# Three seams of a two-block transformer kernel: part-wise waits for weights, products placed inside two mixers, and an end in two token halves

## Time and profile before

| | us |
|---|---|
| median of 3 runs (2592.61 to 2595.39) | 2592.93 |
| the profiled execution | 2590.93 |
| its span, first to last instruction | 2588.8 |
| PE busy | 2524.4 (98%) |
| DVE busy | 1324.3 (51%) |
| ACT busy | 562.1 (22%) |
| POOL busy | 1516.1 (59%) |

### The profile page before, as it was taken

How to read it: one execution, slowest core, us unless ns; L and a number is a source line. 1 busy time by engine, 2 the same in 40 slices (tenths; PEclk the granted TensorE clock), 3 DMA queues, 4 the chain that set the end, 5 groups by cost and what they waited for, 6 DMA issues and landing times.

```text
span 2588.8 us, 31978 instructions
## 1 busy us (share of the span) xinstructions
PE 2524.4 (98%) x11898; PEld 2052.7 (79%) x11898; DVE 1324.3 (51%) x1550; ACT 562.1 (22%) x1022; POOL 1516.1 (59%) x854
## 2 busy tenths in 40 slices
PE   8999999999999999999999999999999978999997
PEld 6888887778888888888887778888887766888886
DVE  5555527656555315555147656555336655655512
ACT  2110014652111001110015552110113554111000
POOL 5666665436666666666665436666664322666664
PEclk9999999999999999999999999999999999999999
DMA  4222221102222222222221112232222110222222
GB/s 154 97 97 97 98 98 66 66 33 98 97 97 97 98 98 84 95 97 97 98 98 66 51 48 98 97 121 97 98 98 114 53 47 33 97 96 93 93 97 76
DMA packets 34915, 228.65 MB, mean 88 GB/s; under 512 B 5392, under 2 KB 6288, under 8 KB 8080
## 3 DMA queue, kind: packets, MB, share of 16 engines
q1 hardware_dynamic: 33392, 225.92, 24.5%
q10 hardware_dynamic: 1440, 1.55, 0.2%
HBM read 225.36 MB, written 2.10 MB: 88 GB/s over the span
## 4 chain that ended last, share of the span: by engine, by line
PE 92%; DVE 4%; ACT 1%; issue 1%; POOL 1%; DMA 0%; SPq 0%; DVEq 0%; POOLq 0%; ACTq 0%
PE bank L571 27%; PE bank L573 27%; PE bank L572 27%; PE bank L700 2%; PE bank L685 1%; PE bank L592 1%; PE bank L669 1%; PE bank L670 1%; POOL wl L542 1%; PE bank L928 1%; PE bank L913 1%; PE bank L586 1%; PE bank L587 1%; DVE ropet L1524 1%; DVE rstd L1425 0%
## 5 line engine op out<-in xcount | busy, mean ns | idle before, releaser
L542 POOL TENSOR_TENSOR wl<-raw,wh 128x1024 fp32r<-128x1024 f32 x412 | 1036.4, 2516 | 34.4
L539 POOL TENSOR_SCALAR wh<-raw 128x1024 fp32r<-128x1024 f32 x412 | 444.4, 1079 | 1012.3 <-PE bank L573 965.4
L571 PE MATMUL bank<-xh,wh 128*128 128x512 f32 x2096 | 818.6, 391 | 0.0
L572 PE MATMUL bank<-xl,wh 128*128 128x512 f32 x2096 | 816.5, 390 | 0.0
L573 PE MATMUL bank<-xh,wl 128*128 128x512 f32 x2096 | 816.3, 389 | 0.0
L573 PEld LDWEIGHTS bank<-xh,wl 128*128 128x128 f32 x2096 | 393.6, 188 | 83.1
L571 PEld LDWEIGHTS bank<-xh,wh 128*128 128x128 f32 x2096 | 393.6, 188 | 80.7
L572 PEld LDWEIGHTS bank<-xl,wh 128*128 128x128 f32 x2096 | 393.7, 188 | 80.6
L571 PE MATMUL bank<-acth,wh 128*128 128x512 f32 x880 | 342.3, 389 | 0.0
L572 PE MATMUL bank<-actl,wh 128*128 128x512 f32 x880 | 342.3, 389 | 0.0
L573 PE MATMUL bank<-acth,wl 128*128 128x512 f32 x880 | 342.3, 389 | 0.0
(11 more groups left out here) (247 smaller groups left out, 2357.4 us busy)
## 6 DMA issues: line engine op xcount, KB each, us to landing
raw<-in_stream SPq DMA_DIRECT2D x206, 1024.0 KB, 4.8
x<-in_x SPq DMA_DIRECT2D x4, 512.0 KB, 7.4
w1k<-in_w1k SPq DMA_DIRECT2D x1, 2048.0 KB, 9.3
out_dram<-x SPq DMA_DIRECT2D x4, 512.0 KB, 2.7
w1v_low<-in_w1v SPq DMA_DIRECT2D x1, 1024.0 KB, 6.9
w1v_high<-in_w1v SPq DMA_DIRECT2D x1, 1024.0 KB, 9.0
...
```

Of the source, the lines that this page charges most:

```text
L539: nc.gpsimd.tensor_scalar(wh[:, h, :, :], src, 1.0, 1.0, ALU.mult, ALU.mult)\
L542: nc.gpsimd.tensor_tensor(wl[:, h, :, :], src, wh[:, h, :, :].bitcast(F32), ALU.subtract).then_inc(split_done, 1)
L571: mm = nc.tensor.matmul(bank, wh[:, slot, k, :], rh, start=start, stop=False)
L572: mm = nc.tensor.matmul(bank, wh[:, slot, k, :], rl, start=False, stop=False)
```

## The change

- `first_units`: PE waits for the high part of unit 1 only, makes six of its high-by-high products, then waits for the low part, makes two low ones, and goes on as before with the rest behind.
- First mixer: at step 1 of the first pair the fill stands before the scores. In the last pair five blocks of the output projection's tile 0 (and a sixth and seventh behind the last transposes) stand between the steps, in the order in which their inputs come; `pooled_map` and what follows it on ACT and DVE move from steps 4 to 8 to steps 1 to 6, through bank 1 alone.
- Second mixer: the units are done at G=44 (`FILL2`: three blocks at 14 steps, and 1, 1, 3, 3 at steps 41 to 44), with the last query unit last. On DVE, `blocks2(0)` stands before the loop and `blocks2(1)` at step 1; `keys2(5)` is cut in two (G=4, 5). The gelu of v goes from G=32 to 30, the transposes to 33 to 36, mean and root from 41/42 to 38, `scale_gated` from DVE at 43 and 45 to ACT at 39, `spatial` from 46 to 49 to 40 to 43, the gelu of u from 50 to 42, `gated` from 52/53 to 45/46, `add_a` from 54/55 to 47/48, `token_sums` from 56 to 49, `norm_rows` from 60 to 52, `normed` from 61/62 to 53/54, `low_mix` from 63 and later to 55/56. The second group's compressed branch goes later: scores from 41/43 to 44/48, minimum 44 to 49, `compressed_normalise` 47 to 51, `compressed_turn` 51 to 54. `queries2(3)` goes from G=38 to 45. At G=56 to 63 stands one block of `out_half(0)` each.
- The end: the last tile's product is made in two halves of 256 tokens in two banks. The squares of the first seven tiles are summed over channels before it is done (`partial_sums`); for each half only column sums of 128x2 go through mean, root and reciprocal, which are spread and transposed to rows. DVE scales six tiles of each half, POOL two (ACT has multiplied their gains in before), and five transfers by SyncE and one by ACT send the halves out.

```diff
-ORDER2 = [12, 13, 14, 8, 15, 16, 17, 9, 4, 5, 6, 10, 7, 0, 11, 1, 2, 3]
+ORDER2 = [12, 13, 14, 8, 15, 16, 17, 9, 4, 5, 6, 10, 7, 0, 1, 2, 3, 11]
...
-FILL2 = tuple(2 + (G in (10, 18, 26, 34, 42, 47)) if G < 49 else 0 for G in range(STEPS2))
+FILL2 = tuple(2 + (G in (9, 12, 15, 18, 21, 24, 27, 29, 31, 33, 35, 37, 39, 40)) if G < 41 else (1, 1, 3, 3)[G - 41]
+              if G < 45 else 0 for G in range(STEPS2))
...
-Q_UNIT = (3, 7, 11, 14)
+Q_UNIT = (3, 7, 11, 17)
 GV_UNIT = (8, 9, 10, 12)
-GU_UNIT = (13, 15, 16, 17)
+GU_UNIT = (13, 14, 15, 16)
...
-          "rows1", "scores0", "scores1", "rows2", "weights0", "blocks0", "blocks1", "gated0", "gated1", "rows3",
-          "gated2", "gated3", "scores2", "scores3", "rows4", "spatial0", "spatial1", "spatial2", "spatial3",
-          "weights1", "rows5", "blocks2", "rows6", "blocks3", "rows7", "sums", "norm_rows"]
+          "rows1", "scores0", "scores1", "rows2", "weights0", "blocks0", "gated0", "gated1", "gated2", "gated3", "rows3",
+          "blocks1", "spatial0", "spatial1", "spatial2", "spatial3", "scores2", "rows4", "scores3", "rows5", "weights1",
+          "blocks2", "rows6", "blocks3", "rows7", "sums", "norm_rows"]
...
-            for part in range(4):
-                sp.wait_ge(fin_done, 2 * part + 2)
-                sp.dma_start(d["out"][:, 2 * part:2 * part + 2, :], x[:, 2 * part:2 * part + 2, :])\
-                    .then_inc(out_done[part], 16)
-            for part in range(4):
+            for part, (half, m, count) in enumerate(((0, LAST_POOL, 6), (0, 0, LAST_POOL), (1, 2, 2), (1, 4, 2), (1, 6, 2))):
+                c = slice(2 * P * half, 2 * P * half + 2 * P)
+                if m < LAST_POOL:
+                    sp.wait_ge(fin_pool, LAST_POOL)
+                else:
+                    sp.wait_ge(fin_done, 6 * half + m + count - LAST_POOL)
+                sp.dma_start(d["out"][:, m:m + count, c], x[:, m:m + count, c]).then_inc(out_done[part], 16)
...
+            for half in range(2):
+                c = slice(2 * P * half, 2 * P * half + 2 * P)
+                pool.wait_ge(fin_gain, LAST_POOL)
+                pool.wait_ge(fin_copy, half + 1)
+                for m in range(LAST_POOL):
+                    nc.gpsimd.tensor_tensor(x[:, m, c], x[:, m, c], sin[:, c], ALU.mult).then_inc(fin_pool, 1)
...
-                def high(e, k):
-                    nc.tensor.matmul(banks[e][:, :], wh[:, e, k, :], xh[:, k, :], start=(k == 0), stop=False)
-                    nc.tensor.matmul(banks[e][:, :], wl[:, e, k, :], xh[:, k, :], start=False, stop=False)
+                def high(e, ks, weights=(wh, wl)):
+                    for k in ks:
+                        for w in weights:
+                            nc.tensor.matmul(banks[e][:, :], w[:, e, k, :], xh[:, k, :], start=(k == 0 and w is wh),
+                                             stop=False)
 
                 def low(e):
                     for k in range(KT):
...
                 pe.wait_ge(split_done, u + 1)
                 for k in range(KT):
                     pe.wait_ge(xh_done, ready * 8 + (k + 1))
-                    high(0, k)
+                    high(0, [k])
+                pe.wait_ge(hi_split, u + 2)
+                high(1, range(6), [wh])
                 pe.wait_ge(split_done, u + 2)
-                for k in range(4):
-                    high(1, k)
+                high(1, range(2), [wl])
                 low(0)
                 sums()
-                for k in range(4, KT):
-                    high(1, k)
+                high(1, range(2, 6), [wl])
+                high(1, range(6, KT))
                 low(1)
...
+                    if t:
+                        pe.wait_ge(ml_done, l * 8 + 6)
                     for h in (0, HD):
-                        mm = nc.tensor.matmul(B[t][h:h + HD, :], poolw[h:h + HD, l, t, :],
+                        mm = nc.tensor.matmul(B[1][h:h + HD, :], poolw[h:h + HD, l, t, :],
                                               padded[h:h + HD, t, PAD:PAD + T], start=True, stop=True)
                     mm.then_inc(poolmm_done, 1)
...
+                def out_blocks(m, ks_, first=False, last=False):
+                    for k in ks_:
+                        start, stop = first and k == ks_[0], last and k == ks_[-1]
+                        if start:
+                            pe.wait_ge(split_done, u0 + (U_PROJ + m) + 1)
+                            if m == 1:
+                                pe.wait_ge(ml_done, l * 8 + 7)
+                        pe.wait_ge(ml_done, l * 8 + (k if 1 < k < 6 else {0: 6, 1: 7, 6: 8, 7: 9}[k]))
+                        mm = split_product(B[m][:, :], m % 2, k, mh1[:, k, :], ml1[:, k, :], start, stop)
+                        if stop:
+                            mm.then_inc(unit_used, 1)
...
-                        if s == 0 and work:
+                        if (s == 0 or g == 1) and work:
                             fill(j, work, FILL[s])
                         scores(g)
-                        if s > 0 and work:
+                        if s > 0 and g != 1 and work:
                             fill(j, work, FILL[s])
+                        if j == PAIRS - 1 and s in OUT_EARLY:
+                            out_blocks(0, OUT_EARLY[s], s == 0)
...
-                        if j == PAIRS - 1 and s in (4, 5):
-                            pooled_map(s - 4)
+                        if j == PAIRS - 1 and s in (1, 4):
+                            pooled_map(s // 4)
                 turn(STEPS - 2)
+                out_blocks(0, (5, 0))
                 turn(STEPS - 1)
-
-                def out_blocks(m, ks_):
-                    unit_blocks(u0 + (U_PROJ + m), m % 2, B[m], ks_, mh1, ml1)
-
-                pe.wait_ge(ml_done, l * 8 + 8)
-                out_blocks(0, range(2))
+                out_blocks(0, (1,))
                 values(HALVES - 1)
                 reciprocal_rows(PAIRS - 1)
-                out_blocks(0, range(2, KT - 1))
-                out_blocks(1, range(2))
-                pe.wait_ge(ml_done, l * 8 + 9)
-                out_blocks(0, [KT - 1])
-                out_blocks(1, range(2, KT))
+                out_blocks(0, (6,))
+                out_blocks(1, (2, 3, 4), True)
+                out_blocks(0, (7,), False, True)
+                out_blocks(1, (5, 0, 1, 6, 7), False, True)
                 for m in range(2, KT):
-                    out_blocks(m, range(KT))
+                    out_blocks(m, range(KT), True, True)
...
-                if G in (22, 24, 41, 43):
-                    compressed_scores((22, 24, 41, 43).index(G))
-                if G in (30, 51):
+                if G in (22, 24, 44, 48):
+                    compressed_scores((22, 24, 44, 48).index(G))
+                if G in (30, 54):
                     compressed_turn(G // 32)
-                if G in (32, 34, 54, 62):
-                    compressed_output((32, 34, 54, 62).index(G))
-                if G in (35, 36, 38, 39):
-                    gated_turn((35, 36, 38, 39).index(G))
-                if 46 <= G < 50:
-                    spatial(G - 46)
-                if G == 56:
+                if G in (32, 39, 56, 62):
+                    compressed_output((32, 39, 56, 62).index(G))
+                if 33 <= G < 37:
+                    gated_turn(G - 33)
+                if 40 <= G < 44:
+                    spatial(G - 40)
+                if G == 49:
                     pe.wait_ge(asum, 3)
-                    pe.wait_ge(evac2, EVACUATED[U_PROJ2 - 1])
+                    pe.wait_ge(evac2, EVACUATED[GU_UNIT[3]])
                     token_sums(0, B[1], gv[:, 0, :], True, True).then_inc(ss2_done, 1)
-                if G == 60:
+                if G == 52:
                     pe.wait_ge(rstd2_done, 1)
                     norm_rows(B[1]).then_inc(rows_done, 1)
+                if G >= 56:
+                    out_half(0, [G - 56])
...
-            out_half(0, range(2))
+            pe.wait_ge(t2_done, STEPS2 + 2)
+            out_half(1, range(2))
             turn2(STEPS2 - 1)
-            out_half(0, range(2, 4))
+            out_half(1, range(2, 4))
             values2(15)
             rows2(7)
-            out_half(0, range(4, 8))
-            pe.wait_ge(t2_done, STEPS2 + 2)
-            out_half(1, range(8))
+            out_half(1, range(4, 8))
...
-            out_half(2, range(5))
+            out_half(2, range(3))
...
+            def last_block(f, half):
+                unit, k = divmod((KT - 1) * FT + f, KT)
+                bank, c = halves[half]
+                if k == 0 and half == 0:
+                    pe.wait_ge(split_done, last + unit + 1)
+                mm = split_product(bank[:, c], unit % 2, k, acth[:, f, c], actl[:, f, c], f == 0, f == FT - 1)
+                if k == KT - 1 and half == 1:
+                    mm.then_inc(unit_used, 1)
+                elif f == FT - 1:
+                    mm.then_inc(half_done, 1)
+
+            def partial_sums():
```

(71 more changed lines are left out.)

239 lines of the change are left out of this document (133 added, 106 removed).

## The result

The changed kernel takes **2563.35 us** (median of 4, 2560.66 to 2564.31); the kernel before, on the same chip, 2592.77 (median of 4, 2591.11 to 2595.39). The ratio is 0.9884, 95% interval 0.9867 to 0.9901: 29.4 us less. The forecast was 2565 with a range of 2556 to 2580. The profiled execution took 2562.65, its span 2560.7.

A forecast was written before the change was run, and what follows sets the result against it. The prediction took PE's one long queue as the bound, busy 2524.4 of 2588.8 us. Its terms 5.1 + 8.8 + 9.9 + 4.5 = 28.3, off the profiled 2590.9, plus 2.0, gave 2565 us, range 2556 to 2580.

The forecast's parts named there:

- Seams, 5.1: Seven seams in `first_units`: low part no longer waited for before the high products, 0.73 us each, 5.1 us less.
- Printed + 0.25: Costing rule for each short PE wait: the printed wait plus 0.25 us.
- First mixer, 8.8: First mixer, two layers: four waits filled, less a new POOL wait and small ones; net 4.4 each, 8.8 us.
- Second mixer, 9.9: Second mixer: start 2.7, loop itself 0.6, after the loop 6.6; together 9.9 us less.
- Steps 44 to 56, 33.7: Second mixer's thin steps: 33.7 us instead of 45.5, steps 45 to 56 DVE bound, DVE above 85% busy.
- After the loop, 6.6: Behind the second mixer's loop: sums 5.4 earlier, norm_rows 1.1 nearer, then ml2 for k=6 limits as before; 6.6 us.
- The end, 4.5: Last tile in halves, matmuls 0.12 apart, half-width tail: 27.4 us instead of 31.9, 4.5 less (-7 to 8).
- Rival C: At the end, the split tile is bound by weight loads, 0.19 us each: 2574 us; chance 0.09.
- B: The second mixer gives nothing, through hand-overs in one PSUM bank and DVE's in-order queue: 2575 us; chance 0.16.
- D: Far better: second mixer's steps 45 to 56 bound by PE, 2557 us; chance 0.09.
- S: Slower: clock falls to 1.2 GHz in the second mixer's bare steps and stays down, 2596 us; chance 0.05.
- E: Nothing to be told from none: seams and first mixer work, end and second mixer lose as much; 2592, chance 0.05.

The follow-up runs named there:

- e1: The kernel before with the edit of the seams (`first_units`) alone: 2587.44 us.
- e9: The changed kernel with the first mixer's five early blocks of output tile 0 put behind the loop's last-but-one turn: 2566.84 us.
- e3: The kernel before with the edits of the second mixer alone: 2583.70 us.
- e8: The changed kernel with one more whole-tile DVE addition, read by nobody, at each of steps 46 to 53: 2568.72 us.
- e5: The changed kernel with unit 2's last w_o block behind unit 3's first two, so GpSimd splits unit 4 later: 2560.37 us.
- e7: The changed kernel with three 512-column matmuls that nobody reads at each of steps 47 to 55: 2564.73 us.
- e6: The changed kernel with the eight output projection blocks of steps 56 to 63 moved together behind the loop, before unit 1: 2563.35 us.
- e12: The changed kernel with one more 128x512 DVE addition, read by nobody, at each of steps 20 to 27: 2566.55 us.

## Why the prediction was right, step by step

Like for like the four parts measured 5.2, 9.9, 8.6 and 4.5, together 28.2 where 28.3 was forecast (the medians give 29.4 for all). That the sum is met so closely is in part luck: the first mixer was taken 1.1 too low and the second 1.3 too high.

**Seams, 5.1.** Right: 5.2 by the traces, 5.6 by e1's median. "Printed + 0.25" (0.72) was the right way to cost a short wait.

**First mixer, 8.8.** Mechanism right, size low by 1.1: 4.95 and 5.0 a layer against 4.4. The new wait for POOL at the unit for m=2 was taken at 0.8; it is there in both layers, and costs 0.65 (printed 0.39, and the matmul behind it comes at 0.33):

```profile
573.36 0.39 PE L602 MATMUL bank<-mh,wl 128*128 128x512 f32 x1
574.14 0.50 PE L600 MATMUL bank<-mh,wh 128*128 128x512 f32 x1 [0.39 <-POOL wl L564]
574.47 0.40 PE L601 MATMUL bank<-ml,wh 128*128 128x512 f32 x1
```

The rest of the difference is in the 0.6 estimated for switching and the last copy, of which 0.2 is left. How the gain is shared is shown for one term alone: e9 bears out the 1.65 + 0.25 given to the three blocks ahead of the value turn (1.85). That the two blocks between the last turns take the other wait, 0.95, fits the traces, in which it is gone wherever they stand, but no run leaves out these two alone.

**Second mixer, 9.9.** A little high: like for like the changed kernel's stages give 8.6 (2.83 - 0.44 + 5.72 + 1.03 - 0.50, the last with a fall of the clock in both, 34.91 in e1 and 35.41), e3's 8.2, its median 9.3.
- The sum has two slips: the terms of steps 57 on add up to 16.2, not 16.5, and those after the loop to 6.5, not 6.6. With both put right the forecast of this part is 10.1.
- Start 2.7: measured 2.83.
- Steps 8 to 43, 111.1: measured 112.8. The waits at spatial() are 4.6 printed (2.42, 1.76, 0.40), under the 5 named. The largest is for ACT's scaled tiles, which the sum did not have: it had the bank's hand-overs only.
- Steps 44 to 56, 33.7: measured 33.9. DVE is on the path, as named (e8: 4.8 of 5.5 us); the sign to look for, DVE over 85% busy, was wrong: 76%. An engine that is idle a quarter of the time can still pass on nearly all of a delay. That this is because each hand-over goes round through it is my reading; e8 doesn't tell it from the amount of work.
- Steps 57 to 62: measured 12.3, 12.5 before, with six of the eight blocks in them. "The loop itself gives 0.6" came out as a loss of 0.4, over 159 us.
- After the loop, 6.6: this is the step that was mis-sized. "So they come 5.4 earlier" is right (5.7), "1.1 nearer" is right (1.03). Wrong is "From there ml2 for k=6 limits as before": from the norm's rows to PE's start behind its last wait for a low part it was 7.30 before (for k=6) and is 8.72 after (for k=7), because of where POOL's split lies. Before, it began 2.9 after the norm's rows, and the last pair of low parts took 2.80; POOL, then DVE before:

```profile
2180.76 1.05 POOL L539 TENSOR_SCALAR wh<-raw 128x1024 fp32r<-128x1024 f32 x1 [4.26 <-PE bank L573]
2181.89 2.68 POOL L542 TENSOR_TENSOR wl<-raw,wh 128x1024 fp32r<-128x1024 f32 x1
```

```profile
2182.93 2.80 DVE L1880 TENSOR_TENSOR ml<-mixed,mh 128x512 fp32r<-128x512 f32 x2
```

After, five blocks of unit 2 stand behind the norm's rows instead of three, the split begins 4.3 after them, and the pair takes 3.99. The forecast looked at PE's order and not at what the end of a unit releases. e5 shows what moving the split out of the way is worth: 3.0 us by the medians, a fall of the clock in some executions included.

**The end, 4.5.** Right in the sum (4.5) and in its parts: 0.12 apart, PE 17.8 us from the tile's first matmul (18.2 forecast), tail 9.5 (9.2). Rival C is refuted by the spacing of 0.12 with a load of its own for each matmul. The forecast cited the Trainium skill ("TensorE: Matmul & The Clock Gate") for its rule that a load overlaps running matmuls only where the row group differs; it stands in the section "The mechanism", ahead of the one named there. Here the row group is the same, and yet load and stream don't add: the 132 matmuls keep 0.12 (124 of their 131 distances; the others hold the sums and rows placed between).

**Rivals.** B (second mixer gives nothing) is refuted by e3's 9.3 us, though its mechanism, a late reader of the shared bank, is part of what is left of the waits (L904 and L929 behind DVE, 2.2 each). D (far better) would have needed PE as the limit of the thin steps; e7, with 6.1 us of PE work added for 1.7, says that it isn't, and e8 that DVE is on the path. S (slower through the clock) is refuted twice, by 0.90 and 1.00 in the changed kernel and by e6's 0.84 and 1.00 without the blocks. E fell with the result.

**What stays open.** What decides whether a pause of PE is followed by a fall of the clock was not settled. What DVE work costs in the filled steps is open too: e12's additions fell in part beside GpSimd's split. So is how 3.1 of the 5.0 us of a first mixer are shared among what e9 leaves in place.
